# Half of a depthwise convolution moved from VectorE to GpSimd, two instructions a tap

## The reference

```python
def conformer_conv(conv_in, dw_w, dw_b, ln_g, ln_b):
    a, gate = conv_in[..., :CONV_CH], conv_in[..., CONV_CH:]      # CONV_CH = 256
    c = a * jax.nn.sigmoid(gate)
    pad = CONV_KERNEL // 2                                        # CONV_KERNEL = 31
    c = lax.conv_general_dilated(
        c, dw_w.reshape(CONV_KERNEL, 1, CONV_CH).astype(c.dtype),
        window_strides=(1,), padding=[(pad, pad)],
        dimension_numbers=('NWC', 'WIO', 'NWC'),
        feature_group_count=CONV_CH) + dw_b.astype(c.dtype)
    c = layer_norm(c, ln_g, ln_b)
    return jax.nn.silu(c)

def second_block(x, mem, positions, ...):
    h = rms_norm_2(x, mix_norm_g[l])
    u = h @ w_in[l]
    c = conformer_conv(conv_in, conv_dw_w[l], ...)
    a = dilated_attention(qkv[0], qkv[1], qkv[2], positions)      # 12 heads of 64
    mixed = jnp.concatenate([rms_norm_2(c, conv_out_g[l]), rms_norm_2(a, attn_out_g[l])], axis=-1)
    x = x + mixed @ w_out[l]
    ...                                                           # cross attention over mem, then 32 experts
```

## Time and profile before

| | |
|---|---|
| median of 3 runs | 2112.65 us (2106.89 to 2113.43) |
| the profiled execution | 2106.04 us, span 2104.2 us |
| TensorE busy | 1906.4 us, 91% of the span |
| VectorE busy | 1133.6 us, 54% |
| ScalarE busy | 891.9 us, 42% |
| GpSimd busy | 17.0 us, 1% |
| mean granted TensorE clock | 0.966 |
| HBM read | 424.68 MB |

### The profile page before, as it was taken

One profiled execution on the slowest core, in us unless ns is written; L12 is line 12 of the kernel. 1 busy time (PEld: TensorE's weight loads), 2 busy tenths in 40 slices (PEclk: granted clock), 3 DMA queues, 4 the chain that ended last, 5 costly groups with the idle time before them and its releaser, 6 DMA issues.

```text
span 2104.2 us, 33676 instructions
## 1 busy us (share of the span) xinstructions
PE 1906.4 (91%) x14126; PEld 1549.9 (74%) x14126; DVE 1133.6 (54%) x1862; ACT 891.9 (42%) x1514; POOL 17.0 (1%) x31
## 2 busy tenths in 40 slices
PE   7999979999999999999899999999999777667766
PEld 4876667778777888899599999997898544444344
DVE  3454756666887788557645667779765111110112
ACT  4333445555766667454444555744845100000001
POOL 0000000000000000000000000000000000000000
PEclk8999999999999999999999999999999988988898
DMA  8222014453555555224035455553246999999996
GB/s 320 80 70 80 1 61 150 150 187 113 180 174 181 195 187 184 82 100 161 1 143 208 162 183 187 186 167 121 74 167 274 419 420 420 419 419 421 420 420 251
DMA packets 91121, 428.00 MB, mean 203 GB/s; under 512 B 11089, under 2 KB 12754, under 8 KB 66002
## 3 DMA queue, kind: packets, MB, share of 16 engines
q1 hardware_dynamic: 78866, 382.51, 48.1%
q10 hardware_dynamic: 12096, 43.26, 6.1%
HBM read 424.68 MB, written 1.05 MB: 202 GB/s over the span
## 4 chain that ended last, share of the span: by engine, by line
PE 64%; DMA 20%; DVE 8%; ACT 5%; issue 2%; SPq 2%; ACTq 0%; POOL 0%; DVEq 0%; POOLq 0%
PE bank L463 41%; PE bank L1600 8%; DMA area<-in_w 5%; DMA HH<-in_w 4%; DMA ring<-in_w 4%; DMA con<-in_w 3%; PE bank L2445 2%; PE bank L478 2%; DVE st L1270 1%; DMA his<-in_w 1%; DMA PPT<-in_w 1%; PE bank L1198 1%; PE bank L2096 1%; SPq L2881 1%; PE bank L937 1%
## 5 line engine op out<-in xcount | busy, mean ns | idle before, releaser
L463 PE MATMUL bank<-HH_r,his_r 128*128 128x256 f32 (+1 forms) x1504 | 502.2, 334 | 1.6 <-DVE ring_r L442 1.6
L463 PE MATMUL bank<-HH_r,ring_r 128*128 128x256 f32 (+1 forms) x1504 | 490.8, 326 | 0.0
L442 DVE TENSOR_TENSOR ring_r<-ring,his_r 128x1024 fp32r<-128x1024 f32 x306 | 373.6, 1223 | 215.8 <-ACT his_r L434 214.3
L463 PE MATMUL bank<-H_r,his_r 128*128 128x256 f32 (+1 forms) x1440 | 472.1, 328 | 0.0
L434 ACT ACTIVATE his_r<-ring 128x1024 fp32r<-128x1024 f32 x306 | 322.5, 1056 | 316.4 <-PE bank L463 232.0
L463 PEld LDWEIGHTS bank<-HH_r,his_r 128*128 128x128 f32 x1504 | 282.3, 188 | 37.2 <-issue 10.5
L463 PEld LDWEIGHTS bank<-HH_r,ring_r 128*128 128x128 f32 x1504 | 282.4, 188 | 24.7
L463 PEld LDWEIGHTS bank<-H_r,his_r 128*128 128x128 f32 x1440 | 270.3, 188 | 29.1 <-issue 2.6
L2461 DVE TENSOR_TENSOR tmp<-tmp,bank 128x128 f32<-128x128 f32 x64 | 18.4, 287 | 384.9 <-ACT tmp L2454 268.0
L2445 PE MATMUL bank<-area,KF 128*32 128x128 f32 x1888 | 89.9, 316 | 43.0 <-DMA area<-in_w 39.7
L463 PE MATMUL bank<-area_r,his_r 128*128 128x256 f32 (+1 forms) x384 | 121.7, 317 | 0.0
(11 more groups left out here) (410 smaller groups left out, 3329.7 us busy)
## 6 DMA issues: line engine op xcount, KB each, us to landing
area<-in_w SPq DMA_DIRECT2D x91, 1024.0 KB, 27.3
ring<-in_w_in SPq DMA_DIRECT2D x102, 512.0 KB, 3.5
ring<-in_w_gate_up SPq DMA_DIRECT2D x88, 512.0 KB, 3.5
ring<-in_w SPq DMA_DIRECT2D x36, 1024.0 KB, 27.4
HH<-in_w SPq DMA_DIRECT2D x26, 1024.0 KB, 27.0
ring<-in_w_down SPq DMA_DIRECT2D x44, 512.0 KB, 3.5
KX<-in_w_mod_rows ACTq DMA_DIRECT2D x28, 512.0 KB, 3.4
VX<-in_w_mod_rows ACTq DMA_DIRECT2D x28, 512.0 KB, 3.5
```

The source lines that it names most:

```text
L442: ve.eng.tensor_tensor(lo_slot(u), stream.slot(u), hi_slot(n).bitcast(F32), ALU.subtract).then_inc(*ve_lo.up(n))
L463: ins = pe.eng.matmul(out, a, b, start=k == 0 and m == 0, stop=end)
```

## The change

The second half of the channels (`CB[:, 1, :]`) is convolved by GpSimd. `ve_conv_taps` makes tap i of half 0 alone, at the same places as before. The new `gp_conv_taps` stands at the end of GpSimd's program: when the second half is gated, it makes tap 0 in one instruction and each further tap in two, the product of the shifted `CP` with the weight into `tmp[0]` or `tmp[1]` in turn, and the addition of it to `CB`. Each product waits for the addition two taps back, each addition for its product. "center" on TensorE waits for the last tap of both. Nothing else is changed; the DMAs and their order are the same.

```diff
--- before.py
+++ after.py
@@ -381,11 +381,11 @@
             "ac_router", "ac_experts", "ac_over",
             "ve_lo", "ve_mod", "ve_filter", "ve_squares", "ve_norm", "ve_out", "ve_rope", "ve_conv", "ve_soft", "ve_cut",
             "ve_angles", "ve_taps", "ve_router", "ve_experts", "ve_over",
-            "gp_start", "gp_cast")}
+            "gp_start", "gp_cast", "gp_taps")}
         (pe_products, pe_mod, pe_sums, pe_filter, pe_conv, pe_scores, pe_turned, pe_values, pe_rope, pe_router, pe_experts,
          pe_over, ac_hi, ac_mod, ac_filter, ac_squares, ac_norm, ac_out, ac_conv, ac_soft, ac_cut, ac_angles, ac_router,
          ac_experts, ac_over, ve_lo, ve_mod, ve_filter, ve_squares, ve_norm, ve_out, ve_rope, ve_conv, ve_soft, ve_cut,
-         ve_angles, ve_taps, ve_router, ve_experts, ve_over, gp_start, gp_cast) = signals.values()
+         ve_angles, ve_taps, ve_router, ve_experts, ve_over, gp_start, gp_cast, gp_taps) = signals.values()
         landed = {n: (sem("d_" + n), 16) for n in ("vec", "x", "con", "dft", "fil0", "fw0", "fil1", "fw1", "cond0", "cond1", "mem", "wr", "br", "late",
                                                    "lw", "pos")}
         banks = Slots([b[:, :] for b in psum])
@@ -1928,17 +1928,33 @@
                                         ALU.mult).then_inc(*ve_norm.up("normed", k))
 
 
+
         def ve_conv_taps(ve, i0, i1):
             for i in range(i0, i1):
-                for j in range(2):
-                    w = vv("dw_w", 31 * j + i)
-                    if i == 0:
-                        ve.wait_ge(*ve_out.at("glu", 1))
-                        ins = ve.eng.tensor_scalar(CB[:, j, :], CP[:, j, 0:N], w, vv("dw_b", j), ALU.mult, ALU.add)
-                    else:
-                        ve.wait_ge(*ve_taps.at("tap", i - 1, j))
-                        ins = ve.eng.scalar_tensor_tensor(CB[:, j, :], CP[:, j, i:i + N], w, CB[:, j, :], ALU.mult, ALU.add)
-                    ins.then_inc(*ve_taps.up("tap", i, j))
+                w = vv("dw_w", i)
+                if i == 0:
+                    ve.wait_ge(*ve_out.at("glu", 1))
+                    ins = ve.eng.tensor_scalar(CB[:, 0, :], CP[:, 0, 0:N], w, vv("dw_b", 0), ALU.mult, ALU.add)
+                else:
+                    ve.wait_ge(*ve_taps.at("tap", i - 1))
+                    ins = ve.eng.scalar_tensor_tensor(CB[:, 0, :], CP[:, 0, i:i + N], w, CB[:, 0, :], ALU.mult, ALU.add)
+                ins.then_inc(*ve_taps.up("tap", i))
+
+
+        def gp_conv_taps(gp):
+            gp.wait_ge(*ve_out.at("glu", 1))
+            gp.wait_ge(*landed["vec"])
+            for i in range(31):
+                product = tmp[i % 2][:, 0:N]
+                w = vv("dw_w", 31 + i)
+                if i == 0:
+                    gp.eng.tensor_scalar(CB[:, 1, :], CP[:, 1, 0:N], w, vv("dw_b", 1), ALU.mult, ALU.add).then_inc(*gp_taps.up("tap", 0))
+                    continue
+                if i > 2:
+                    gp.wait_ge(*gp_taps.at("tap", i - 2))
+                gp.eng.tensor_scalar(product, CP[:, 1, i:i + N], w, None, ALU.mult).then_inc(*gp_taps.up("product", i))
+                gp.wait_ge(*gp_taps.at("product", i))
+                gp.eng.tensor_tensor(CB[:, 1, :], CB[:, 1, :], product, ALU.add).then_inc(*gp_taps.up("tap", i))
 
 
 
@@ -1972,7 +1988,8 @@
             if h == 3:
                 out = banks.take((ve_taps, ("centered", 1)), "center")
                 pe.wait_ge(*banks.emptied("center"))
-                pe.wait_ge(*ve_taps.at("tap", 30, 1))
+                pe.wait_ge(*ve_taps.at("tap", 30))
+                pe.wait_ge(*gp_taps.at("tap", 30))
                 for j in range(2):
                     ins = pe.eng.matmul(out[:, 0:N], ones[:, :], CB[:, j, :], start=j == 0, stop=j == 1)
                 ins.then_inc(*pe_sums.up("center"))
@@ -2826,6 +2843,7 @@
             gp_norm_mod(gp, "ffn0", 512)
             gp_norm_mod(gp, "mix1", 512)
             gp_norm_mod(gp, "ffn1", 256)
+            gp_conv_taps(gp)
 
         def sync_program(sp):
             def weights(i):
```

## The result

The kernel became slower: median 2116.88 us of 20 runs against 2110.35 us of 20 runs of the kernel before, ratio 1.003, 95% interval 1.0022 to 1.0037. In microseconds that is +6.5, between 4.6 and 7.8 by the interval. The profiled execution has a span of 2114.0 us, 9.8 more than before; part of that is scatter, since the mixer's heads already began 2.3 us later. A measure that is free of it is the stretch on VectorE from the first head's eviction (L1896) to the fifth attention mask (L1267): everything that the change touches lies between.

The account below looks back on a forecast made before the run. VectorE was taken to bound the mixer's heads and first attention heads. 11.0 us less work against about 20 us of standing still gave +9 on the 2112.65 median, about 2121.5 us; range 2104 to 2137.

Parts of the forecast that it names:

- What binds, and that the loss moves the end one to one: Mixer's heads and first attention heads: VectorE binds, and a microsecond won or lost there moves the end by about one.
- 11.0 us come free: VectorE loses 31 tap instructions, 12.2 us; 11 dependent neighbours give 1.2 us back, leaving 11.0 us less.
- The ceiling of 7.1 us: Most there is to win: TensorE's 4.5 us idle time in the stretch plus 2.6 us from its half clock.
- The 2.6 us for the clock: TensorE's 5 us at half clock behind its wait for an attention head's probabilities costs 2.6 us with its edges.
- The engines take turns where both read SBUF: A VectorE instruction with two SBUF inputs and a reading GpSimd instruction exclude each other; VectorE stands still about 20 us.
- full 1.01 us a tap: Upper price for VectorE by the skill's rule: it stands still for GpSimd's whole product, 0.40 us, and sum, 0.61.
- The price of a tap, 0.71 to 1.01 us and three quarters of it: VectorE's standstill per GpSimd tap; 31 taps 22 to 31 us, three quarters exposed, so 16.5 to 23, taken as 20.
- GpSimd's chain, 1.07 us a tap and 32.5 us in all: GpSimd's product 0.40 us, sum 0.61, plus waits; undisturbed it ends at 1426.4, 43 us before "center" needs it.
- The neighbours that read one tensor are untouched: VectorE's evictions, masks, maxima and scalings, a quarter of its stretch, read one SBUF tensor or none and are not held.
- No hindrance: Rival: the engines do not hinder each other, VectorE's 11.0 us come free, time 2105.6 us; chance 0.24, little hindrance included.
- Starving: Rival: VectorE wins every turn, GpSimd finishes late and TensorE waits at "center"; about 2122 us, chance 0.14.
- The clock: Rival: with head turns of 5 us or more TensorE drops to 1.2 GHz; +20 to +28, 2133 to 2140 us, chance 0.12.

Follow-up runs that it names:

- e1: The change with GpSimd's chain cut to tap 0, the second half's taps 1 to 30 left out; ratio 0.9973 against the kernel before.
- e2: The kernel before, both halves on VectorE, plus GpSimd's 61 instructions into an unused place that "center" also waits for; ratio 1.008.
- e3: As e1, but GpSimd then fills a 512-column tile with zeros 91 times, only writing; ratio 0.9975 against the kernel before.
- e4: The change without GpSimd's sums: tap 0 and 30 products only, second half's taps 1 to 30 missing; ratio 0.9976 against the kernel before.
- e5b: The change without GpSimd's products: tap 0 and 30 sums written where nothing reads, taps 1 to 30 missing; ratio 1.0015 against the kernel before.
- e8: Only second-half taps 1 to 11 leave VectorE: ScalarE products, GpSimd sums, each sum waiting for VectorE's split; ratio 0.999 against the kernel before.
- e9: As e8 without the wait for the split, each sum starting when ScalarE's product is there; ratio 0.9986 against the kernel before.
- e10: As e9, with second-half taps 22 to 30 also moved to ScalarE products and GpSimd sums; ratio 0.9982 against the kernel before.
- e7: The change with the second half's products made by ScalarE, GpSimd only adding, whole computation kept; ratio 1.0015 against the kernel before.

## Why the prediction was right, and where its sizes were off

- *The time.* The forecast 2121.5 lies 4.6 us above the measured 2116.88. Half of that, 2.3 us, is the base: the three runs shown had a median of 2112.65, the twenty of this comparison 2110.35. The other half is +9 against +6.5.
- *What binds, and that the loss moves the end one to one.* Right. VectorE stayed busy throughout; the stretch grew 5.3 us and the median 6.5.
- *11.0 us come free.* Right: dependent taps stand 0.52 us apart and not 0.395, 0.125 a neighbour where 0.11 was taken, and in e1 VectorE is busy 10.5 us less.
- *The ceiling of 7.1 us.* Too high: 5.4 to 5.7 (e1). The 2.6 us for the clock were nearly right, 2.3 came back; of the 4.5 us of idle time 1.4 stayed, since the wait for the probabilities stays.
- *The engines take turns where both read SBUF.* Right for what VectorE loses, and shown from three sides: e2 with nothing saved, e1 with nothing done, e3 with the same busy time and no reads. The Trainium skill (SBUF — State Buffer, "Who interferes with whom") says the same of instructions with two SBUF inputs, and that a GpSimd instruction that only writes does not meet them; the trace agrees, with splits of 1.46 us mean in the change and 1.22 in e3. It does not bear out the prediction's "full 1.01 us a tap" by that rule: a tap cost 0.50, and a product of 0.92 us held VectorE for about 0.2.
- *The price of a tap, 0.71 to 1.01 us and three quarters of it.* Too high: this is the term that made +9 of what was +6.5. Measured: 15.5 us of standing still, 0.50 a tap, under the range of 16.5 to 23 of which 20 was taken. 15.5 less 10.5 to 11.0 is +4.5 to +5.0, and the stretch shows +5.3. The turns of e4 and e5b give 0.14 and 0.35 us for the two steps. By the prediction's bounds, three quarters of 0.25 to 0.40 and of 0.46 to 0.61, they were to cost 0.19 to 0.30 and 0.35 to 0.46: the product is under its range, the sum at the low end of its own. The 0.25 us was read off one cast that happened to collide; in e4's chain one product of each three costs nothing and the others about 0.2 us (L1921 0.60 us for 0.42, L1927 0.70 for 0.48).
- *GpSimd's chain, 1.07 us a tap and 32.5 us in all.* Wrong, and that it did no harm is luck. Even after VectorE's taps were nearly done a tap took 1.71 us from start to start, about 1.0 from product to sum and 0.71 from sum to product, so 53 us unhindered, and 73 as it ran (1396.25 to 1468.98). The cast of 0.40 us was no measure for a product with a weight from SBUF: 0.92 in the rows, while the sum's 0.73 was near the 0.61 taken. The chain was done 9 us before "center", where the prediction had it done 43 us before when undisturbed. A chain longer by more than 9 us would have begun to set the end.
- *The neighbours that read one tensor are untouched.* Right for those that read PSUM and for the maximum L1270 (0.69 us in both kernels), wrong for the scaling L1249 (1.27 us for two against 0.62). The section of the Trainium skill named above exempts an instruction with one SBUF input only "outside the 2-port perf modes", a condition that the prediction left out. Whether L1249 ran in such a mode no run here shows, so why it was held stays open. The other way round, L1919 was counted among those that are held and kept 0.41 us in the change, where only the end of a product fell beside it; beside a sum, in e8, it took 0.57.
- *The rivals.* No hindrance: refuted by e2. Starving: refuted, GpSimd got its turn after each of VectorE's instructions that it met, two taps a turn. The clock: refuted; with TensorE busy 26.38 of 30 us it stayed at 1.00, and in e5b, where a turn has the 5 us that the rival asked for, with 10.46 busy of 15 (1415 to 1430 us). In the change it dipped only behind the same head's wait, and less: 0.84 and 0.82 in two stretches of 5 us, where it had been 0.87 and 0.50.

## What to carry to other kernels

An engine that is idle is not free if it reads through what the binding engine reads through. Before moving work to GpSimd, count the instructions of the binding VectorE that have two inputs in SBUF, and let GpSimd's reads fall beside those that read PSUM; a read of GpSimd's that starts inside a long instruction of VectorE waits itself and costs VectorE nothing. With the products on ScalarE, moving 11 and 20 of the 31 taps gained about 3 and 4 us (e9, e10), where moving all of them lost 3 (e7), and 6.5 with the products on GpSimd too. A step that frees 11 us of the binding engine is also worth no more than the next engine lets it: leave the work out once and measure that first.

## What the runs showed of the hardware

- A GpSimd addition of 128x256 f32 took 0.72 to 0.74 us unhindered, a product with a per-partition weight 0.92, a cast of the same size 0.40, a fill of 128x512 0.53. ScalarE made the same product in 0.49.
- A VectorE instruction with two SBUF inputs that starts beside a running GpSimd sum is held until the sum ends, up to 0.55 us; beside a fill it is not held at all, and beside a product for about 0.2 us.
- A GpSimd sum that starts beside a running split is held instead (1.00 us for 0.73 in e9), and the split keeps 1.22.
- GpSimd and VectorE fell into a fixed pattern: in the heads each turn of the change repeats to 0.01 us (splits at 1411.09, 1415.68, 1420.26).
